# Host layout of inputs, weights and tables, and a first projection taken in pieces, in a fused two-block transformer kernel

## The reference

```python
# first block
h = rmsnorm(x, norm_mix_g)                      # x: (256, 1024)
z = h @ w_in                                    # 1024 -> 7176 columns: hq hf hi hg fq fk fv ff mq gates
f = lb + (1 - lb) * sigmoid(hf)                 # lb: softmax of hgrn_lb_logits
y_a = hgrn2(silu(hq), f, hi, hg)                # chunked scan, 4 heads
y_b = forgetting_attention(fq, fk, fv, ff)      # 8 heads, causal
y_c = attention(mq, rmsnorm(mem, norm_mem_g) @ mem_kv_w)   # 4 heads into 256 memory tokens
merged = gates[0] * (y_a @ w_br_hgrn) + gates[1] * (y_b @ w_br_fox) + gates[2] * (y_c @ w_br_mem)
x = x + merged @ w_out
a, v = split(rmsnorm(x) @ ffn_w_up)
x = x + (gelu(causal_conv3(a)) * v) @ ffn_w_down
# second block
x = x + 0.5 * swiglu(rmsnorm(x))
x = x + token_mixer(rmsnorm(x))  # 4 differential heads and 8 dilated heads; their scores get a bias
                                 # rel_bias[t5_bucket(distance), head]; dilated ones the log of a count too
x = x + 0.5 * swiglu(rmsnorm(x))
return rmsnorm(x, final_norm)
```

## Time and profile before

| | us |
|---|---|
| median of 3 runs | 1046.16 |
| the three runs | 1048.93, 1046.16, 1045.85 |
| the profiled execution, its own time | 1050.62 |
| span of its profile | 1048.5 |
| TensorE busy in the span | 1006.0 (96%) |
| VectorE busy | 666.6 (64%) |
| ScalarE busy | 477.8 (46%) |
| GpSimd busy | 80.7 (8%) |

### The profile page before, as it was taken

The page is one execution under the profiler, slowest core; times in us unless marked ns, Lnnn a source line. Parts: engine busy times, 40 slices in busy tenths (PEclk is TensorE's granted clock), DMA queues, the critical chain, the costliest instruction groups (busy, mean ns, idle before and its releaser), DMA issues. The chain is left out here.

```text
span 1048.5 us, 17492 instructions
## 1 busy us (share of the span) xinstructions
PE 1006.0 (96%) x7506; PEld 958.7 (91%) x7506; DVE 666.6 (64%) x848; ACT 477.8 (46%) x573; POOL 80.7 (8%) x202
## 2 busy tenths in 40 slices
PE   4999998999999999999999999999997899999996
PEld 4999998989999999999899999989997899999995
DVE  3578865685876866666675555556667366555554
ACT  4455555554435544444543434444434254434343
POOL 0010104532140000000000000000002000000001
PEclk9999999999999999999999999999999699999999
DMA  8656545342456555464556565654333146565641
GB/s 280 203 162 190 179 155 162 125 157 96 146 165 223 189 189 202 166 209 166 182 170 199 179 199 178 200 163 161 121 121 121 47 162 215 164 201 177 197 146 40
DMA packets 143558, 175.77 MB, mean 168 GB/s; under 512 B 4661, under 2 KB 130777, under 8 KB 143482
## 3 DMA queue, kind: packets, MB, share of 16 engines
q1 hardware_dynamic: 138794, 168.30, 49.4%
q10 hardware_dynamic: 4688, 6.36, 1.9%
HBM read 173.58 MB, written 4.22 MB: 170 GB/s over the span
## 5 line engine op out<-in xcount | busy, mean ns | idle before, releaser
L336 PE MATMUL ps<-hTh,wh 128*128 128x256 f32 x1512 | 431.3, 285 | 7.5 <-DVE wl L1227 6.9
L1227 DVE TENSOR_TENSOR wl<-raw,wh 128x2048 fp32r<-128x2048 f32 (+1 forms) x156 | 356.6, 2287 | 115.2 <-ACT wh L841 114.9
L336 PE MATMUL ps<-hTl,wh 128*128 128x256 f32 x1512 | 428.2, 283 | 0.0
L336 PE MATMUL ps<-hTh,wl 128*128 128x256 f32 x1512 | 428.1, 283 | 0.0
L841 ACT ACTIVATE wh<-raw 128x2048 fp32r<-128x2048 f32 (+1 forms) x158 | 299.5, 1900 | 177.9 <-PE ps L336 177.4
L336 PEld LDWEIGHTS ps<-hTh,wh 128*128 128x128 f32 x1512 | 289.7, 192 | 11.1 <-DVE wl L1227 6.7
L336 PEld LDWEIGHTS ps<-hTl,wh 128*128 128x128 f32 x1512 | 289.7, 192 | 1.4
L336 PEld LDWEIGHTS ps<-hTh,wl 128*128 128x128 f32 x1512 | 289.6, 192 | 0.2
L336 PE MATMUL ps<-wh,yTh 128*128 128x512 f32 (+1 forms) x328 | 123.9, 378 | 1.4 <-DVE BIGT L1625 1.3
L336 PE MATMUL ps<-wl,yTh 128*128 128x512 f32 (+1 forms) x328 | 124.5, 380 | 0.0
L336 PE MATMUL ps<-wh,yTl 128*128 128x512 f32 (+1 forms) x328 | 122.6, 374 | 0.0
(11 more groups left out here) (253 smaller groups left out, 811.6 us busy)
## 6 DMA issues: line engine op xcount, KB each, us to landing
raw<-in_ffn_w_up SPq DMA_DIRECT2D x44, 1024.0 KB, 5.3
raw<-in_w_in SPq DMA_DIRECT2D x40, 1024.0 KB, 5.3
raw<-in_ffn_w_down SPq DMA_DIRECT2D x33, 1024.0 KB, 5.1
raw<-in_ffn_w_gate SPq DMA_DIRECT2D x22, 1024.0 KB, 5.3
raw<-in_w_out SPq DMA_DIRECT2D x8, 1024.0 KB, 5.0
raw<-in_mem_kv_w SPq DMA_DIRECT2D x4, 1024.0 KB, 5.0
scr_f<-scr_r ACTq DMA_DIRECT2D x1, 3072.0 KB, 15.3
raw<-in_w_br_hgrn SPq DMA_DIRECT2D x2, 1024.0 KB, 5.0
```

The lines of the kernel that those rows point to most:

```text
L336: ins = pe.matmul(o, l(k), r(k), start=first and k == ks[0] and j == 0, stop=last and k == ks[-1] and j == 2)
L1227: dve.tensor_tensor(wl[j % NS][:, 0:n], raw[j % NR][:, 0:n], wh[j % NS][:, 0:n].bitcast(F32), ALU.subtract).then_inc(w_lo, 1)
```

## The change

The host now lays out the arrays. x and mem are sent a second time, turned (`x_turned`, `mem_turned`), so that `hTh` and `hTl` are made straight from a tile `XT` in on-chip memory and TensorE turns neither. Each weight unit is one contiguous block whose partition holds 8 KB in a row (before: eight runs of 1 KB). Vectors come as columns, the masks as bytes, the lambdas and the forget bias already spread over partitions. The bias table comes as the 16 finished maps, 128 by 4096 numbers, and a map of log counts, `times`; GpSimd negates the first and subtracts the second (two new instructions, L1961 and L1964 of the changed kernel). The lookup matmuls, the store, the skewed copy and its read are gone.

The first two units are loaded, split and multiplied in pieces: unit 0 in four pieces with the four of x, unit 1 in two. x itself, needed for the squares, is loaded after unit 2.

```diff
-            pe.wait_ge(c_in, 16)
-            pe.wait_ge(grow_in, 16 * 6)
-            t = take("gt", T.take())
-            pe.transpose(t[:, 0:48], grows[:, :], ident[0:48, 0:48]).then_inc(ps_full[at["gt"][0]], 1)
-            norm_turn(0, 2)
-            norm_turn(0, 3)
-            norm_pair(("hf", 0), ("hf", 1), 0)
-            for u in range(2):
-                rows_out(("hq", u), WF)
+            i, bs = U["hf", 0], [WF.take(), WF.take()]
+            ts = [take(("hf", 0, m), bs[m]) for m in range(2)]
+            for n in range(4):
+                pe.wait_ge(*((w0_lo, n + 1) if n < 3 else (w_lo, 1)))
+                for m in range(2):
+                    ins = three(ts[m][:, 0:256], weight_left(i, 256, m * 128), right(hT_at), (2 * n, 2 * n + 1), n == 0,
+                                n == 3, (lambda k: (xt_lo, k + 2)) if m == 0 else None)
...
+            rows_out(("hq", 0), WF)
+            spread(0)
+            rows_out(("hq", 1), T)
...
-            pe.wait_ge(rel_neg, 2)
-            for j in range(2):
-                b = T.take()
-                t = take(("toep", j), b)
-                pe.matmul(t[0:16, 0:384], rel[:, :], oneh[:, 384 * j:384 * j + 384], start=True,
-                          stop=True).then_inc(ps_full[b], 1)
...
-                for p in (2 * half, 2 * half + 1):
-                    turn(("xm", p), XM, p, 1024)
-            toks_out(("mk", 0), W, ready=lambda k: free(("xm", k // 2)))
+            toks_out(("mk", 0), W, ready=lambda k: (mt_lo, k + 2))
...
+            def gained_hi(p, g, made):
+                for k in (2 * p, 2 * p + 1):
+                    c = slice(k * 256, k * 256 + 256)
+                    act.activation(hTh[:, c], XT[:, c], ACT.Copy, scale=gain_col(g, k)).then_inc(made, 1)
...
+            for p in range(4):
+                act.wait_ge(xt_in[p], 16)
+                gained_hi(p, 0, xt_hi)
+                c = slice(p * 512, p * 512 + 512)
+                act.wait_ge(w0_in[p], 16)
+                act.activation(wh[0][:, c], raw[0][:, c], ACT.Copy).then_inc(*((w0_hi, 1) if p < 3 else (w_hi, 1)))
...
-                act.wait_ge(f_st, 16)
-                act.dma_start(BIGT[:, 0:4096].rearrange("p (m n) -> p m n", m=16),
-                              bass.AP(scr_f.tensor, 127, [[383, 128], [128 * 384, 16], [1, 256]])).then_inc(toep_in, 16)
+                act.dma_start(BIGT[:, 0:4096], I["bias"]).then_inc(bias_in, 16)
+                act.wait_ge(pv_done, 12)
+                act.dma_start(times, I["times"]).then_inc(bias_in, 16)
...
+            dve.wait_ge(c_in, 16)
+            norm_end(0)
+            spread_out(0)
+            pair_scaled(E0[:, 0:512], ("hf", 0))
+            rows_scaled(E0[:, 512:1024], ("hf", 1))
             lo_to(3)
...
-            dve.tensor_copy(VT[:, :], bank[at["vt"][0]][:, 0:NROWS]).then_inc(*emptied("vt"))
-            dve.tensor_copy(masks[:, :], BIGT[:, 0:896]).then_inc(masks_in, 1)
...
             pool.wait_ge(zero_set, 4)
+            pool.wait_ge(bias_in, 32)
+            pool.tensor_scalar(BIGT[:, 0:4096], BIGT[:, 0:4096], -1.0, None, ALU.mult).then_inc(bias_neg, 1)
+            pool.wait_ge(bias_neg, 1)
+            dil = BIGT[:, 2048:4096].rearrange("p (h n) -> p h n", h=8)
+            pool.tensor_tensor(dil, dil, times.unsqueeze(1).to_broadcast([128, 8, 256]), ALU.subtract).then_inc(bias_made, 1)
...
+            for p in range(4):
+                c = slice(p * 512, p * 512 + 512)
+                sp.dma_start(XT[:, c], I["x_turned"][:, c]).then_inc(xt_in[p], 16)
+                sp.dma_start(raw[0][:, c], I["units"][0, :, c]).then_inc(w0_in[p], 16)
+            for p in range(2):
+                c = slice(p * 1024, p * 1024 + 1024)
+                sp.dma_start(raw[1][:, c], I["units"][1, :, c]).then_inc(w1_in[p], 16)
+            load(2)
+            sp.dma_start(v3(X[:, :]), I["x"][0].rearrange("(t p) n -> p t n", p=128)).then_inc(x_in, 16)
...
+                    sp.wait_ge(xt_lo, 8)
+                    sp.dma_start(XT[:, :], I["mem_turned"]).then_inc(mt_in, 16)
```

More of the change, by code:

```diff
@@ L139, in build @@
         X, Hn = sb("X", 2048), sb("Hn", 2048)
-        grows, GT = sb("grows", 128, parts=48), sb("GT", 48)
+        XT, GT = sb("XT", 2048), sb("GT", 48)
         C = sb("C", 544)
         masks = sb("masks", 7 * 128, U8)
[L143 to L146, removed]
+        VT = sb("VT", NROWS)
         BIGT = sb("BIGT", 6144)
@@ L386, in norm_turn, with spread @@
                 turn(("n", k, p), X, p, 1024)
+            def spread(k):
+                b = T.take()
+                t = take(("rb", k), b)
+                pe.wait_ge(diag_made, 2 * k + 2)
+                if k == 0:
+                    pe.wait_ge(ones_set, 1)
+                for m in range(2):
+                    ins = pe.matmul(t[:, m * 128:m * 128 + 128], ones[:, :], diag[:, m * 128:m * 128 + 128], start=True,
+                                    stop=True)
+                ins.then_inc(ps_full[b], 1)
             def norm_pair(key0, key1, k):
@@ new lines, in pe_program @@
+            unit_end[i] = full(("hf", 0, 1))
+            i, b = U["hf", 1], WF.take()
+            t = take(("hf", 1), b)
+            for m in range(2):
+                for n, ks in enumerate((EIGHT[0:4], EIGHT[4:8])):
+                    if m == 0:
+                        pe.wait_ge(*((w_lo, 2) if n else (w1_lo, 1)))
+                    ins = three(t[:, m * 256:m * 256 + 256], weight_left(i, 256, m * 128), right(hT_at), ks, n == 0, n == 1)
+            ins.then_inc(ps_full[b], 1)
+            unit_end[i] = full(("hf", 1))
@@ L1969, in sp_program @@
-            for i in range(1, NR):
-                load(i)
-            row_load("cw", I["ffn_conv_w"][0].rearrange("j (m p) -> (j m) p", p=128), 66)
-            row_load("cb", I["ffn_conv_b"][0].rearrange("(m p) -> m p", p=128), 22)
-            row_load("lb", I["hgrn_lb_logits"].rearrange("l (h p) -> (l h) p", p=128), 8)
-            for name, g in (("fq", "fox_q_norm_g"), ("fk", "fox_k_norm_g")):
-                for j in range(2):
-                    row_load(name, I[g], 1, (64 * j, 64 * j + 64))
@@ L1985, in sp_program @@
+            sp.dma_start(VT[:, :], I["columns"]).then_inc(vt_in, 16)
+            sp.dma_start(lam4, I["lambdas"]).then_inc(lam_in, 16)
+            sp.dma_start(fb, I["forget_bias"]).then_inc(fb_in, 16)
+            sp.dma_start(masks[:, :], I["masks"]).then_inc(masks_in, 16)
             for i in range(NR, NU):
@@ new lines, in constants, with laid_out, turned, as_columns @@
+    far = np.minimum(31, 16 + (np.log(np.maximum(d, 1) / 16) / np.log(128.0) * 16).astype(np.int64))
+    row = np.where(d < 0, -1, np.where(d < 16, d, far))
+    times = (d <= 128) * 1 + (d % 4 == 0) + (d % 16 == 0)
+    log_times = np.where((d < 0) | (times == 0), 0.0, np.log(np.maximum(times, 1)))
+    return c, m.reshape(128, 896).astype(np.uint8), row, times, log_times.astype(np.float32)
+def laid_out(inputs):
+    import numpy as np
+    I = {name: np.asarray(a) for name, a in inputs.items()}
+    c, masks, row, times, log_times = constants()
+    weights = weight_plan(I)
+    plan = [(key, w.shape[0] // 128 * w.shape[1]) for key, w in weights]
+    units = np.zeros((len(plan), 128, 2048), np.float32)
+    for i, (_, w) in enumerate(weights):
+        units[i, :, 0:plan[i][1]] = w.reshape(-1, 128, w.shape[1]).transpose(1, 0, 2).reshape(128, -1)
+    def turned(x):
+        return x.T.reshape(-1, 128, x.shape[0]).transpose(1, 0, 2).reshape(128, -1)
+    def as_columns(v):
+        return np.reshape(v, (-1, 128)).T
+    columns = np.zeros((128, NROWS), np.float32)
+    columns[:, 0:66] = as_columns(I["ffn_conv_w"][0])
+    columns[:, 66:88] = as_columns(I["ffn_conv_b"][0])
+    columns[:, 88:96] = as_columns(I["hgrn_lb_logits"])
+    for name, g in (("fq", "fox_q_norm_g"), ("fk", "fox_k_norm_g"), ("mq", "mem_q_norm_g"), ("mk", "mem_k_norm_g"),
+                    ("hg", "hgrn_norm_g"), ("sub", "subln_gain_2")):
+        columns[:, ROWS[name]] = np.resize(I[g][0], 128)
+    bias = np.zeros((128, 16, 256), np.float32)
+    for n in range(16):
+        seen = row >= 0 if n < 8 else (row >= 0) & (times > 0)
+        bias[:, n, :] = np.where(seen, I["rel_bias_2"][np.maximum(row, 0), n], np.float32(-BIG))
+    lambdas = np.concatenate([I[g][0] for g in ("lambda_q1_2", "lambda_k1_2", "lambda_q2_2", "lambda_k2_2")])
+    arrays = {"x": I["x"], "mem": I["mem"], "final": I["final_norm_2"], "units": units, "x_turned": turned(I["x"][0]),
+              "mem_turned": turned(I["mem"][0]), "gains": np.concatenate([as_columns(I[g][0]) for g in GAINS], 1),
+              "columns": columns, "bias": bias.reshape(128, 4096), "times": log_times,
+              "lambdas": np.tile(lambdas, (128, 1)), "forget_bias": np.tile(I["fox_f_bias"][0], (128, 1)),
+              "const": c, "masks": masks}
+    return plan, {name: np.ascontiguousarray(a) for name, a in arrays.items()}
```

182 lines of the change are left out of this document (70 added, 112 removed).

## The result

The changed kernel takes 1056.8 us (median of 4 runs, 1054.94 to 1059.08) beside 1047.55 for the kernel before in the same comparison: a ratio of 1.009, 95% interval 1.006 to 1.012, so 9 us slower. The forecast was 1047.2, 1.0 above the 1046.16 known then for the kernel before, with a range of 1039.5 to 1052.0 and a chance of 0.20 for slower by over 0.3%. It was wrong. The profiled execution took 1054.94 us, the fastest of the four, and has a span of 1053.1 us.

What follows compares the result with a forecast made beforehand. TensorE, busy 1006.0 of 1048.5 us, was taken as the bound. Start -7.3, lookups -0.7, bias pass +6.2, clock +1.4 and +1.4 gave +1.0 us on 1046.16: 1047.2, range 1039.5 to 1052.

Steps and rivals of the forecast that it cites:

- the negation: GpSimd negating 4096 bias columns before the second norm: taken as 3.8 us, between bounds of 3.8 and 10.5.
- rival C: GpSimd before the second norm: negation at two-input pace, 6.7 us more, 1053.9 in all; chance 0.10.
- the bias pass: GpSimd at the norm before the first feed-forward: negation and subtraction (4.7 us) make TensorE wait 6.2 us for `diag`.
- the start: Loading and splitting in pieces: first product at 6.5 us, 7.3 us won in all by the lookup matmuls.
- the clock: TensorE running slow behind two new rests, before `hq` 1 and at the bias pass: 1.4 us lost each.
- The mechanism: At the norm, VectorE steps with two on-chip operands stand until GpSimd's instruction is done: TensorE waits 6.2 us.
- the new stall: Before `hq` 1: unit 3's low part queued on VectorE behind `RB`, TensorE waits 4.1 us.
- the lookups: Lookup matmuls removed, 1.4 us, only 0.7 won; TensorE's wait before the first level products grows instead.
- the turning of mem: About 1.8 us of TensorE work removed, wins nothing: the wait in `mk` 0 grows to about 3.6 us.
- A: Norm before the first feed-forward: the bias pass costs nothing, 6.6 us faster, 1039.6; chance 0.23.
- B: Bias lands early (328.3) and the clock stays up: 4.5 us faster, 1041.7; chance 0.15.
- D: Loads at the start: pieces pay a fixed cost one after the other, start loses about 17 us, 1064; chance 0.02.

Runs made afterwards that it cites:

- before_pass: Kernel before, plus two GpSimd instructions of the same size at the same place (128x4096 times 1.0, 128x2048 product with ones): 1063.95 us, ratio 1.0138.
- no_pass: Changed kernel without GpSimd's negation and subtraction of the bias maps, load kept: 1043.62 us, ratio 0.9953 against the kernel before.
- quarters: Changed kernel with the GpSimd pass cut into 4 negations and 2 subtractions of 128x1024: 1050.64 us, ratio 1.0021 against the kernel before.
- runs1k: Changed kernel with weight units laid out in eight blocks again, runs of 1 KB instead of 8 KB: 1059.42 us, ratio 1.0103 against the kernel before.
- lo3: Changed kernel with unit 3's low part made on VectorE before `RB` is copied out: 1052.89 us, ratio 1.0035 against the kernel before.
- chunks: Changed kernel with the GpSimd pass cut into 16 negations and 8 subtractions of 128x256: 1046.42 us, ratio 0.9979 against the kernel before.
- chunks_lo3: Changed kernel with the diffs of chunks and lo3 together: 1040.18 us, ratio 0.9927 against the kernel before.
- best: Changed kernel with lo3's diff, ScalarE negating in feed-forward steps 2 to 5, GpSimd subtracting in pieces of 256 from step 6: 1038.34 us, ratio 0.9909.
- late: Changed kernel with the uncut GpSimd pass started behind the feed-forward's fifth product of gate and value: 1047.88 us, ratio 0.9997 against the kernel before.
- sub_only: Changed kernel without the negation, GpSimd's subtraction kept: 1043.84 us, ratio 0.9964 against the kernel before.
- whole: Changed kernel with units 0 and 1 loaded, split and multiplied whole: 1063.08 us, ratio 1.0148 against the kernel before.

## Why the prediction was wrong

**The failing step is the choice of 3.8 us for the negation.** The prediction said "It has one input, so I take 3.8", at the pace of a memset, between bounds of 3.8 and 10.5. It took 10.56, the upper bound, which stood for the two-input pace. A memset reads nothing; the rows had no reading one-input instruction of GpSimd, and so no row favoured the lower end. That was rival C, with a chance of 0.10. Of the 8.4 us between the forecast's +1.0 and the trace's +9.4, the bias pass has 5.0 (11.2 instead of 6.2), the start 1.9 and the clock 1.8. Even C's 1053.9 is 3 us short of the measured 1056.8, so the negation alone doesn't explain the miss. The Trainium skill ("GPSIMD Engine Reference", "Engine selection") calls one-input elementwise work roughly line rate; the estimate of 3.5 us that the prediction made from it is a third of the measured 10.56, and the measurement decides.

**The mechanism was right.** VectorE stood behind GpSimd as the earlier trace rows had shown; before_pass and no_pass show it from both sides, 14 us each. The subtraction was forecast at 4.7 and took 4.50. The wait was 10.7 and not C's 12.9. The main reason is the load: in the changed kernel the bias was issued at 318.39 and the counts were there at 326.87, 8.5 us later, where the forecast had 9.8 (321.22 to 331). The subtraction was 0.2 shorter, and 2.0 us of chain were left behind it where the forecast had 2.45.

**The clock was undersized:** 1.4 us for each of two rests, 2.8. The table shows 2.2 us behind the stall at `hq` 1, 1.5 behind `mk` 0 and 0.9 behind `diag`, 4.6 in all. These are one execution's: over the traces the same three places cost 1.3 to 2.2, nothing to 2.1, and 0.9 to 2.0. So 1.4 for a rest was of about the right size, and what the term lacked is the third place. The one at `mk` 0 I had not thought of: I priced the longer wait at zero because the turning's time went into it. It is no fixed price: the clock fell at `mk` 0 in the changed kernel, no_pass, quarters and runs1k, and not in lo3, chunks, chunks_lo3, best, late, sub_only and whole. Behind the 4.1 of `hq` 1 it fell in every trace that has this stall, for 3.4 or 6.8 us.

**The start won less:** 5.4 us to `hq` 1 instead of 7.2. The first product came 0.76 later than forecast (7.26), because the first piece of unit 0 was there at about 5.8 and not at 5.1, and 24 matmuls ran slow instead of 16, 8 x 0.09 = 0.7. That leaves 0.3 unexplained. The profiled execution even had the earliest start of all: in the five other traces of the same start (no_pass, chunks, quarters, late, sub_only) the first product comes at 7.6 to 8.5 us and `hq` 1 is 4.0 to 5.1 us ahead of before. Its order was right, including the new stall (4.1 forecast, 4.10 measured), which lo3 removed whole.

**Right as forecast:** the lookups, 1.4 won and 0.8 given back (1.4 and 0.7), at a wait of 1.52 for the first levels; the turning of mem, 1.4 won and, but for 0.4, given back in waits of 1.76 + 1.68 = 3.44 (3.6 forecast). These two are read from the traces only; no run took them apart.

**The other rivals.** A (the pass costs nothing) is out by the wait of 10.7 us. B (early landing, clock up) is half true: in the old count the counts landed at 329.7 (326.87 plus the 2.8 us that the kernel was ahead), between B's 328.3 and the forecast's 331, but the clock fell. D (pieces pay one after the other) is out: the first product starts at 7.26 us, and the whole units of the run above cost 6 us more.

Together: -5.4 (start) - 1.4 + 0.8 (lookups) - 0.4 (the rest up to `mk` 0) + 2.2 + 1.5 + 0.9 (clock) + 11.2 (pass) = +9.4.

## What to carry to other kernels

Where an instruction of unknown pace sits in front of a chain of small dependent steps, bound it from instructions that read and write as it does, and give the upper end the weight when only that end has them. Put large GpSimd passes where VectorE's consumers have work in store, cut them into pieces, or give them to an engine that idles there. A wait that grows costs its length and can cost a slow clock behind it (at the 4.1 us before `hq` 1 in 8 traces of 8, at `mk` 0 in 4 of 11), so a wait "in place of removed work" is not free.

## What the runs showed of the hardware that was not expected

- A GpSimd instruction with one input over 128x4096 takes 10.56 us, 2.6 ns per column, which is more than the 2.2 of the subtraction with two inputs (4.50 for 2048); ScalarE takes 1.05 for 1024.
- VectorE isn't shut out over the whole of every GpSimd instruction. In quarters, nine steps of 0.16 us ran between 332.0 and 333.8, while a negation of 1024 columns was under way by its span; in the changed kernel the first step came free 1.7 us before the negation's end and the next stood until it, and in before_pass the same two steps did so 1.71 us before and at the end. In quarters the step before those nine came free at 331.96, again 1.71 us before the end of its negation. Behind the subtraction, which has two inputs, the step ended only with it (329.78 and 329.76 in sub_only). GpSimd's spans are rough, so whether the shutting out ends early or the span does is open.
- GpSimd stands behind VectorE as well: in chunks a negation of 256 columns took 2.77 us instead of 0.85 beside a low part of 2.28, in late the subtraction 5.35 instead of 4.50.
- The same waits of TensorE (1.76 and 1.68 us at 225.93 and 229.30; 1.77 and 1.67 in lo3) were followed by the lower clock in one execution and not in another, and before_pass had 3.4 us of it at 235 us, where the kernel before had none. What decides is open.
- With 8 KB runs the queues moved 391 GB/s between 8 and 12.5 us (409 in lo3, 411 in no_pass); in runs1k, the same kernel with 1 KB runs, 360, and in the kernel before 355.
